# Which quad of a cached-attention phase takes which K, V or U weight tile

## What is computed

```
h = rmsnorm(x, norm1_g)
z = h @ w_in                       # 2048 x 4096, split into q, k, v, u (1024 each)
a = attend(q, k, v)                # prompt: causal with ALiBi; samples: 2048 cached keys each,
                                   # read through a page table, best 3 blocks of 256 keys per query head
p = pool_mixer(u)                  # causal means over 2, 4, 8, 16 tokens, then a grouped matmul
x = x + concat(a, p) @ w_out
x = x + (silu(h2 @ w_gate) * (h2 @ w_up)) @ w_down     # h2 = rmsnorm(x), inner width 5632
y = rmsnorm(x)
```

## Time and profile before

| what | value |
|---|---|
| median of 3 runs | 1473.88 us (1471.16 to 1475.2) |
| the profiled execution's own time | 1475.53 us |
| its span in the trace | 1473.7 us, mean granted clock of TensorE 0.981 |
| TensorE busy | 1406.9 us (95%) |
| TensorE weight loads busy | 1301.7 us (88%) |
| VectorE busy | 902.7 us (61%) |
| ScalarE busy | 501.9 us (34%) |
| GpSimd busy | 109.3 us (7%) |
| DMA | 334.41 MB, mean 227 GB/s |

### The profile page before, as it was taken

How to read it: one execution, slowest core, us unless ns; L and a number is a source line. 1 busy time by engine, 2 the same in 40 slices (tenths; PEclk the granted TensorE clock), 3 DMA queues, 4 the chain that set the end, 5 groups by cost and what they waited for, 6 DMA issues and landing times.

```text
span 1473.7 us, 34086 instructions
## 1 busy us (share of the span) xinstructions
PE 1406.9 (95%) x13894; PEld 1301.7 (88%) x13894; DVE 902.7 (61%) x1352; ACT 501.9 (34%) x663; POOL 109.3 (7%) x184
## 2 busy tenths in 40 slices
PE   6998999999898999999999999999999999999986
PEld 4987777767556799999999999999999999999986
DVE  4778777767777555687454555555555546464635
ACT  4422121122134234543343434343333333333333
POOL 2127500000010001300000000000000000000003
PEclk9999999999899999999999999999999999999998
DMA  5888999999999855655555555555555555555531
GB/s 182 261 323 303 347 400 402 402 398 393 389 387 361 291 170 181 190 168 196 166 170 160 168 167 162 169 164 163 170 160 168 168 161 170 165 163 170 162 124 65
DMA packets 164280, 334.41 MB, mean 227 GB/s; under 512 B 10223, under 2 KB 54440, under 8 KB 163599
## 3 DMA queue, kind: packets, MB, share of 16 engines
q1 hardware_dynamic: 164183, 333.06, 66.6%
HBM read 328.10 MB, written 5.27 MB: 226 GB/s over the span
## 4 chain that ended last, share of the span: by engine, by line
PE 81%; SPq 8%; DVE 4%; DMA 3%; issue 2%; ACT 1%; POOL 0%; POOLq 0%; ACTq 0%; DVEq 0%
PE banks L1424 24%; PE banks L1425 24%; PE banks L1426 24%; PE banks L1537 4%; SPq L424 3%; SPq L428 2%; DMA vpage<-in_cache_v 2%; PE banks L1519 2%; SPq L446 2%; PE banks L1430 2%; DVE kpage L886 1%; DMA kpage<-in_cache_k 1%; PE banks L1553 1%; DMA vec<-in_pool_scale 1%; SPq L416 1%
## 5 line engine op out<-in xcount | busy, mean ns | idle before, releaser
L844 DVE TENSOR_TENSOR w_lo<-w_raw,w_hi 128x1024 fp32r<-128x1024 f32 x360 | 440.2, 1229 | 409.9 <-ACT w_hi L583 408.7
L1424 PE MATMUL banks<-hh,w_hi 128*128 128x288 f32 x2176 | 646.1, 297 | 4.3 <-issue 1.8
L1425 PE MATMUL banks<-hl,w_hi 128*128 128x288 f32 x2176 | 644.5, 296 | 0.0
L1426 PE MATMUL banks<-hh,w_lo 128*128 128x288 f32 x2176 | 642.5, 295 | 0.5 <-issue 0.5
L583 ACT ACTIVATE w_hi<-w_raw 128x1024 fp32r<-128x1024 f32 x360 | 379.0, 1058 | 683.5 <-PE banks L1426 461.5
L1424 PEld LDWEIGHTS banks<-hh,w_hi 128*128 128x128 f32 x2176 | 410.7, 189 | 22.1 <-issue 20.1
L1425 PEld LDWEIGHTS banks<-hl,w_hi 128*128 128x128 f32 x2176 | 410.9, 189 | 1.3 <-issue 1.2
L1426 PEld LDWEIGHTS banks<-hh,w_lo 128*128 128x128 f32 x2176 | 409.7, 188 | 0.4 <-issue 0.4
L1424 PE MATMUL banks<-ah,w_hi 128*128 128x288 f32 x704 | 208.7, 296 | 9.5 <-DVE af L1264 5.4
L1426 PE MATMUL banks<-ah,w_lo 128*128 128x288 f32 x704 | 209.4, 297 | 0.0
L1425 PE MATMUL banks<-al,w_hi 128*128 128x288 f32 x704 | 209.1, 297 | 0.0
(11 more groups left out here) (193 smaller groups left out, 651.0 us busy)
## 6 DMA issues: line engine op xcount, KB each, us to landing
kpage<-in_cache_k SPq DMA_DIRECT2D x128, 512.0 KB, 7.9
vpage<-in_cache_v SPq DMA_DIRECT2D x128, 512.0 KB, 7.1
w_raw<-in_w_gate SPq DMA_DIRECT2D x88, 512.0 KB, 3.6
w_raw<-in_w_up SPq DMA_DIRECT2D x88, 512.0 KB, 3.6
w_raw<-in_w_down SPq DMA_DIRECT2D x88, 512.0 KB, 3.7
w_raw<-in_w_in SPq DMA_DIRECT2D x64, 512.0 KB, 9.3
w_raw<-in_w_out SPq DMA_DIRECT2D x32, 512.0 KB, 4.0
xs<-in_x_prompt SPq DMA_DIRECT2D x2, 1024.0 KB, 7.3
```

Of the source, the lines that this page charges most:

```text
L844: V.tensor_tensor(w_lo[:, s, :], w_raw[:, s, :], w_hi[:, u, :].bitcast(F32), ALU.subtract).then_inc(lo_ready, 1)
L1424: PE.matmul(o, wh, xh[:, c, :], start=start and i == 0, stop=False)
L1425: PE.matmul(o, wh, xl[:, c, :], start=False, stop=False)
L1426: last = PE.matmul(o, wl, xh[:, c, :], start=False, stop=stop and i == len(chunks) - 1)
```

## The change

Two tiles move from the first step to the sixth. The table `KVU_COUNT` gives the number of tiles by quad: 2, 1, 1, then 2 in each of 18 quads, then 3 and 3. So quad 0 takes tiles 2 and 3, quad 1 tile 4, quad 2 tile 5, quad n from 3 to 20 takes tiles 2n and 2n+1, quad 21 takes 42, 43 and 44, quad 22 takes 45, 46 and 47, and quad 23 none. Blocks now end in the second and fourth quad of a step (in quad 0 for the first). VectorE's `take_block` calls move accordingly, the second one of a step behind `osb_high`. In quad 21 a block ends between tiles 43 and 44: `split_at_block` gives a head (42, 43), which TensorE runs ahead of the values, and a tail (44) behind them. On VectorE the low part of that tail comes behind `turn_k` of the third quad and `take_block`.

```diff
+KVU_COUNT = (2, 1, 1) + (2,) * 18 + (3, 3)
+KVU_FIRST = 2
+KVU_AT = [range(KVU_FIRST + sum(KVU_COUNT[:n]), KVU_FIRST + sum(KVU_COUNT[:n + 1])) for n in range(len(KVU_COUNT))]
+KVU_AT += [range(0)] * (NQUADS * KVU_STEPS - len(KVU_AT))
+BLOCKS_IN = [[k // 4 for k in tiles if k % 4 == 3] for tiles in KVU_AT]
+def split_at_block(n):
+    first = BLOCKS_IN[n][0] if BLOCKS_IN[n] and KVU_AT[n][-1] % 4 != 3 else -1
+    return [k for k in KVU_AT[n] if k // 4 == first], [k for k in KVU_AT[n] if k // 4 != first]
...
 SyncE
-            load_kvu(4)
-            load_kvu(5)
+            for k in KVU_AT[1]:
+                load_kvu(k)
...
-                for k in (2 * n + 6, 2 * n + 7):
-                    if k < KVU_TILES:
+                if n + 2 < len(KVU_AT):
+                    for k in KVU_AT[n + 2]:
                         load_kvu(k)
...
 VectorE
+            def slot_ends(n):
+                for m in BLOCKS_IN[n]:
+                    take_block(m)
+
             for i in range(KVU_STEPS):
-                lo_kvu(4 * i + 1)
+                n = NQUADS * i
+                lo_kvu(KVU_AT[n])
...
-                take_block(2 * i)
-                lo_kvu(4 * i + 2)
+                slot_ends(n)
+                head, tail = split_at_block(n + 1)
+                lo_kvu(head or tail)
                 turn_k(i, 2)
-                lo_kvu(4 * i + 3)
+                slot_ends(n + 1)
+                lo_kvu(tail if head else ())
+                lo_kvu(KVU_AT[n + 2])
                 turn_k(i, 3)
-                take_block(2 * i + 1)
-                lo_kvu(4 * i + 4)
+                slot_ends(n + 2)
+                lo_kvu(KVU_AT[n + 3])
...
                 turn_k(i + 1, 0)
                 if i:
                     osb_high(i - 1)
+                slot_ends(n + 3)
...
 TensorE
+                    head, tail = split_at_block(NQUADS * i + j)
+                    for k in head:
+                        kvu_tile(k)
                     if i:
                         values(i - 1, j - 1)
-                    kvu_pair(4 * i + j + 1)
+                    for k in tail:
+                        kvu_tile(k)
```

More of the change, by code:

```diff
@@ L470, in _ @@
                     load_k_page((k - 6) // 4, (k - 6) % 4)
-            for k in range(4):
+            for k in range(KVU_FIRST):
+                load_kvu(k)
+            for k in KVU_AT[0]:
                 load_kvu(k)
@@ L622, in _, with hi_kvu @@
                 hi(tile_at(4 + k))
[L624 to L627, removed]
+            def hi_kvu(tiles):
+                for k in tiles:
+                    hi(tile_at(T_KVU + k))
             def save_comb(b):
@@ L692, in mixed @@
                 copy(hh[:, c, :], nrm[:, r % 2, :]).then_inc(y_hi, 1)
-            hi_kvu(0)
+            hi_kvu(range(KVU_FIRST))
             for i in range(KVU_STEPS):
-                hi_kvu(4 * i + 1)
+                hi_kvu(KVU_AT[NQUADS * i])
                 if i >= 2:
@@ L702, in _ @@
                 for j in range(1, NQUADS):
-                    hi_kvu(4 * i + j + 1)
+                    hi_kvu(KVU_AT[NQUADS * i + j])
                 if i == KVU_STEPS - 1:
@@ L875, in x_taken, with lo_kvu @@
                 V.tensor_copy(xT[:, c, :], XB[c % 3][:, 0:T]).then_inc(x_ready, 1)
[L877 to L880, removed]
+            def lo_kvu(tiles):
+                for k in tiles:
+                    lo(tile_at(T_KVU + k))
             def turn_k(i, j, pages_=range(4)):
@@ L912, in _ @@
                     turn_k(0, 0)
-                    lo_kvu(0)
+                    lo_kvu(range(KVU_FIRST))
                 if k % 8 == 7:
@@ L1628, in _ @@
                     combine(i - 2)
-                kvu_tile(8 * i + 2)
+                kvu_tile(KVU_AT[NQUADS * i][0])
                 if i:
                     joint_max(i - 1)
-                kvu_tile(8 * i + 3)
+                kvu_tile(KVU_AT[NQUADS * i][1])
                 if i:
```

## The result

The changed kernel takes 1479.86 us (median of 7 runs, 1478.28 to 1483.9); the kernel before took 1473.88 (median of 7, 1471.16 to 1476.24). The ratio is 1.0045, 95% interval 1.0033 to 1.0057: slower by 5 to 8 us. The prediction was 1478.4 in a range of 1471.0 to 1482.5, 4.5 above before. So the sign and most of the size came out, though the outcome lies just beyond the 0.3% within which the largest single chance (0.48) stood. The profiled execution took 1479.65 us, with a span of 1477.9, 4.2 above the span of before.

A forecast was written before the change was run, and what follows sets the result against it. The prediction took TensorE to bound step 0, and the pages and tiles brought by DMA the later steps. Its terms, -5.3 + 0.5 + 10.0 - 0.7 = +4.5 us on the median 1473.88, gave 1478.4 us, range 1471 to 1482.5.

The forecast's parts named there:

- TensorE binds step 0, DMA the later ones: Whole kernel: TensorE busy 37.2 of 40.5 us in step 0; later steps bound by pages and tiles at 400 GB/s.
- Step 0 pays 5.3 us: Step 0 loses two tiles; quad 4's logits start at 126.3 in place of 131.61, with VectorE coming last.
- Steps 1 to 4 carry the gain unchanged, and the moved block ends are free: Steps 1 to 4: loads follow consumption, so step 0's gain is kept; moved block ends cost 0, bounds 0 to 1.
- Step 5 costs 10.0 us: Step 5: 1.5 for K's delay, 2.0 for `take_block` and low part, 6.5 for two tiles; 7 to 13.
- 1.5 us for the transfer ahead of K: Step 5: tile 44's load goes ahead of quad 22's K, whose last page lands 1.47 us later.
- Step 6 gives 0.7 back: Step 6: shorter load queue as TensorE comes later, so 0.7 us is taken back; 0 to 2.
- +0.5 for more low clock: End of step 0: TensorE's longer wait may bring a longer slow stretch, 0 to 1.5 us; 0.5 taken.
- B: Rival: DMA, relieved until step 5, brings quad 22's K up to 2.9 us earlier; +1.6, 1475.5; chance 0.20.
- A: The forecast's own sum over all steps: 1478.4 us, own range 1475.5 to 1481.5; chance 0.50.
- C: Rival: added tiles fill step 5's waits if quad 22's transposes end before 360; -3.0, 1469 to 1471; chance 0.12.
- D: Rival: quad 3's K lands no earlier, behind 4 MB of V, so step 0 doesn't pay; +8, 1482; chance 0.18.
- The weighed rules: Two skill rules not followed: half the low-clock time lost (sum near 9); 3.2 us per tile transfer (sum 6.2).

The follow-up runs named there:

- e3_stubs: Kernel before, with most of the load, splitting and matmuls of tiles 5 and 7 left out: 1468.25 us, ratio to before 0.9968.
- e6_step3: e1_block_first with the two tiles moved to step 3 (quads 13 and 14 take three each): 1472.7 us, ratio to before 0.9997.
- e1_block_first: Changed kernel, but in quad 21 VectorE takes the block and makes tile 44's low part ahead of quad 22's transposes: 1473.45 us, ratio to before 1.0002.
- e5_control: Changed kernel's code with two tiles in each of quads 0 to 22, the order of the kernel before: 1473.62 us, ratio to before 1.0000.
- e2_k_first: Changed kernel, but SyncE asks for tile 44 behind quad 22's K pages: 1478.1 us, ratio to before 1.0033.
- e9_warm: Changed kernel with 50 added matmuls on TensorE between quad 21's values and tile 44: 1477.73 us, ratio to before 1.0048.
- e8_v_later: Changed kernel, but SyncE asks for quad 1's V pages behind quad 4's K, not ahead of tile 4: 1479.78 us, ratio 1.0049.

## Why the prediction was right, and where it was off

- **TensorE binds step 0, DMA the later ones.** Right. Two tiles left out of step 0 and put nowhere give 4.6 us (e3_stubs); two tiles added in step 3 cost 3 us there, not 6.5 (e6_step3).
- **Step 0 pays 5.3 us.** Too much: 2.4 in the profiled execution and 2.2 in that of e1_block_first, 3.2 to 3.9 in the eight others with tiles 4 and 5 alone in quads 1 and 2 or with stubs. Quad 2's logits came as forecast (107.0 in times of before). The step that failed is the next one: that with two tiles fewer ahead the loads asked for behind quad 1's logits land earlier. In times of before, quad 3's last K page was to land at 112.2 and landed at 114.5, and tile 7 was to land near 115 and was taken up at 117.5; in the kernel before they had 114.6 and 117.5, so neither gained anything. Taking the median of another group of four, 5.0 us, for its last page explains only 0.6 of this, since the last page of that group took 5.6 us and this one 7.13. The tile mattered more than the page. Its low part was to be done at 117.3, from where VectorE's 9.0 us lead to quad 4's logits. It was done at 119.8, and in the eight other traces at 118.9 to 119.5: that is the missing 1.4 to 2.1 us. The slow logits behind the K page (4.54 us) added 0.53 us to it in the changed kernel and in e1_block_first. VectorE's way from the logits taken to the transposes was as described (8.9 us).
- **Steps 1 to 4 carry the gain unchanged, and the moved block ends are free.** Right in the main: 157.0 us against 157.4 in steps 2 to 4. Together steps 1 to 4 are 2.1 us shorter, just past the 2 us that the prediction had named as a sign of being wrong. Step 1 is 1.6 of it, but e5_control, with the order of before, has 48.3 there too: that execution of before had a low clock in quad 5's logits (4.23 us).
- **Step 5 costs 10.0 us.** 9.5 in the traces. Tile 44's wait was forecast at 6.3 us and took 6.5, ended by `lo` (L858, L844 before) as named, and from quad 23's logits to step 6 the chain took 13.9 us in both kernels. What lies between was split otherwise than forecast: the low clock (2.7 us on quad 22's logits and values) fell on tile 44 instead, 1.6 us, and the logits ran at full speed. So, counted from quad 20's logits, quad 22's came 8.9 us later and not 6.7, and quad 23's only 0.6 more and not 3.3. e1_block_first shows the order on VectorE to be the cause of the wait, and shows more: there the third tile does fill the wait for K, so the order is worth 6.4 us, not only the 2.0 us of `take_block` and low part that I booked apart from the tiles' own time.
- **1.5 us for the transfer ahead of K.** K's last page landed 2.1 us later than before, counted from quad 20's logits, and 1.8 of that is gone in the trace of e2_k_first. The medians can't confirm it.
- **Step 6 gives 0.7 back.** 0.9 from quad 24 to 31, and TensorE's wait for a V page there, 0.7 us in the kernel before, is gone. But e5_control, with the order of before, is 1.5 us shorter in this stretch, so that the size came out is partly luck.
- **+0.5 for more low clock.** Open. By the traces the whole is +4.2 (span), close to the forecast of 4.5; by the medians it is +6.0. The profiled execution of before lay 1.65 above its median, that of the changed kernel 0.2 below its own, so the pair understates the change. That 4.2 lies so near 4.5 is partly luck: step 0 paid 2.9 less than forecast, and most of what steps 1 to 4 seem to give in return belongs to one execution of before. Against the medians 1.5 us are missing, about what step 0 fell short by in the eight other traces. Low clock could be a part as well: the mean granted clock was 0.985 over 28 runs of before and 0.9826 over 7 of the changed kernel, about 7 us more at half the clock (an estimate, 2 x 0.0024 x 1475). It costs time only where TensorE is the bound. At tile 44 it is, and e9_warm shows 1.5 us. Ahead of quad 24 TensorE's wait grew from 0.7 to 4.5 us and the logits behind it took 4.53 us in place of 2.75, and yet quad 25's came 13.2 us behind them in both kernels.
- **The rivals.** B (DMA gets ahead and brings quad 22's K early) fails: K landed 2.1 us later than before when both traces are counted from quad 20's logits (27.0 us against 24.9), as A had it. C has the mechanism of e1_block_first, not of this kernel: its point of decision, the transposes' end before 360, was missed by 7 us counted from quad 20's logits. Its time isn't that of e1_block_first either, which equals the kernel before where C had 3 us less. D's condition held, quad 3's K landed no earlier than before, and its size of step 0 was nearer than A's in the profiled execution; but its reason, the V pages ahead, is refuted by e8_v_later, and the first wait of step 1 was ended by VectorE, not by a page.
- **The weighed rules.** That lost time is half the low-clock time (the Trainium skill, "TensorE: Matmul & The Clock Gate", Terms) fits tile 44: 4.9 us at a mean of 0.65 against 3.4 at 1.00, where the rule gives 0.35 x 4.9 = 1.7. It doesn't fit as a price of the whole kernel, as quad 24's logits show. The fit of 2.0 us plus bytes over 436 GB/s for a single transfer ("DMA: Bandwidth & Descriptors" in the Trainium skill, Anatomy of one DMA), which the page gives for transfers that GpSimd issues and not SyncE, would have made the transfer 3.2 us; the K page moved by 1.8.

## What to carry to other kernels

When work is moved to fill a wait on one engine, follow its inputs through the in-order list of every other engine: here the filling tile's own input stood behind the very transposes whose lateness it was to cover, and moving two items ahead of them was worth 6.4 us. Work taken out of a stretch bound by one engine and put into one bound by DMA cost about its transfer there (3 us for two tiles), but the whole kernel gained nothing that the measurement could tell. When an engine is relieved, ask which load sets the next step, and whether that load is asked for any earlier: step 0 paid 3 to 4 of 6.5 us because the next two tiles landed nearly as late as before. And a saving that is smaller than the spread of single executions should be read from the same stretch in several traces: two of ten had another chain of waits in step 0 than the rest.

## What the runs showed of the hardware that I had not expected

K pages of 512 KB asked for 1.1 us apart (104 to 108 us, DMA at 235 GB/s between 104 and 110) landed 2.3, 2.2 and 2.7 us apart (quad 3 of the changed kernel: issues to landing 3.40, 4.63, 5.49 and 7.13 us). While DMA moved 400 GB/s they landed 1.3 apart (quad 22's pages of before: 9.1 to 9.6 us each). So the last page of a group gained little from a relieved queue: 7.13 us against the 7.4 of the kernel before, which had a tile more ahead of it. Where DMA had stood idle (0 GB/s from 135 to 137 us of before) the four pages took 3.3, 4.5, 5.4 and 5.6 us. And 50 matmuls that nobody needed, put into a wait of 6.5 us, kept TensorE at its full clock and made the next 24 matmuls 1.5 us faster.
